# Gathering each expert's tokens with the residual's columns as the stationary operand, in a two-block fp32 network

## What is computed

```python
cap = EC_CAPACITY_FACTOR * n // N_EXPERTS            # 2 * 256 / 16 = 32 tokens for each expert
logits = h @ w_router + b_router
aff = softmax(logits)
gate, idx = top_k(swapaxes(aff, 1, 2), cap)
xs = h[idx]                                          # gather: 16 x 32 rows of 1024
a = einsum('becd,edf->becf', xs, w_gate)             # w_gate, w_up: 1024 x 2048 for each expert
u = einsum('becd,edf->becf', xs, w_up)
y = einsum('becf,efd->becd', silu(a) * u, w_down) * gate
out = zeros.at[idx].add(y)                           # scatter back to the 256 tokens
```

## Time and profile before

| | us |
|---|---|
| median of 3 runs (1554.5 to 1554.9) | 1554.64 |
| the profiled execution, in all | 1554.04 |
| its span from first to last instruction | 1552.2 |
| TensorE busy in the span | 1198.4 (77%) |
| TensorE's weight loads | 696.7 (45%) |
| VectorE | 614.4 (40%) |
| ScalarE | 425.8 (27%) |
| read from memory | 548.36 MB, 354 GB/s over the span |

### The profile page before, as it was taken

The page is one execution under the profiler, slowest core; times in us unless marked ns, Lnnn a source line. Parts: engine busy times, 40 slices in busy tenths (PEclk is TensorE's granted clock), DMA queues, the critical chain, the costliest instruction groups (busy, mean ns, idle before and its releaser), DMA issues.

```text
span 1552.2 us, 18204 instructions
## 1 busy us (share of the span) xinstructions
PE 1198.4 (77%) x7368; PEld 696.7 (45%) x7368; DVE 614.4 (40%) x1041; ACT 425.8 (27%) x644; POOL 36.9 (2%) x62
## 2 busy tenths in 40 slices
PE   7999999999999999976666665665655665665665
PEld 5888977887887899721111111111111111111112
DVE  3786789889777876511011011011011011110111
ACT  3665357786554674300000000000000000000001
POOL 0000000010001000000000000000000000000000
PEclk9999999999999999988777787787878877777788
DMA  9876877687756666999999999999999999999996
GB/s 362 284 263 216 308 245 246 231 307 235 273 183 209 215 220 245 390 432 430 430 432 430 430 431 432 430 432 432 432 429 431 432 430 431 431 430 430 432 432 276
DMA packets 78323, 550.62 MB, mean 355 GB/s; under 512 B 5032, under 2 KB 5320, under 8 KB 61856
## 3 DMA queue, kind: packets, MB, share of 16 engines
q1 hardware_dynamic: 75168, 541.08, 86.2%
q0 software_dynamic: 2784, 8.08, 1.7%
q10 hardware_dynamic: 288, 0.30, 0.1%
HBM read 548.36 MB, written 1.61 MB: 354 GB/s over the span
## 4 chain that ended last, share of the span: by engine, by line
PE 43%; DMA 36%; DVE 12%; ACT 4%; issue 3%; SPq 0%; DVEq 0%; ACTq 0%; POOL 0%
PE ps L610 41%; DMA b<-in_w_down 34%; DVE b L1535 6%; ACT b L1171 3%; PE ps L614 3%; DVE b L1552 2%; DVE b L2265 1%; ACT b L1173 1%; DVE b L2206 1%; DMA b<-in_w_in 1%; DMA b<-in_w_ada 1%; DVE b L2212 1%; DVE b L1545 0%; ACT L1171 0%; DVE b L1566 0%
## 5 line engine op out<-in xcount | busy, mean ns | idle before, releaser
L610 PE MATMUL ps<-b,b 128*32 128x512 f32 (+7 forms) x6922 | 1130.3, 541 | 300.0 <-DMA b<-in_w_up 117.3
L610 PEld LDWEIGHTS ps<-b,b 128*32 128x32 f32 (+2 forms) x6922 | 640.9, 159 | 750.5 <-issue 456.5
L1171 ACT ACTIVATE b<-ps 128x512 f32<-128x512 f32 (+3 forms) x165 | 92.2, 559 | 868.7 <-PE ps L610 560.7
L1535 DVE TENSOR_TENSOR b<-b,b 128x1024 fp32r<-128x1024 f32 (+5 forms) x254 | 277.1, 1091 | 98.1 <-ACT b L1171 78.9
L1171 ACT ACTIVATE b<-b 128x1024 fp32r<-128x1024 f32 (+6 forms) x219 | 219.1, 1001 | 213.9 <-PE ps L610 161.2
L2255 DVE TENSOR_TENSOR b<-b,ps 128x512 f32<-128x512 f32 x16 | 11.0, 687 | 395.6 <-issue 382.3
L2265 DVE TENSOR_TENSOR b<-b,ps 128x1024 f32<-128x1024 f32 x28 | 34.2, 1222 | 304.3 <-PE ps L610 304.3
L614 PE MATMUL ps<-b,b 128*128 128x128 f32 (+1 forms) x360 | 69.7, 322 | 38.4 <-DVE b L1566 23.5
L614 PEld LDWEIGHTS ps<-b,b 128*128 128x128 f32 (+1 forms) x360 | 45.8, 168 | 88.9 <-DVE b L1566 36.4
L1552 DVE SCALAR_TENSOR_TENSOR b<-b,b,b 128x512 f32<-128x512 f32 (+3 forms) x50 | 63.2, 1263 | 4.3 <-ACT b L1171 0.5
L1535 DVE TENSOR_TENSOR b<-ps,b 128x512 f32<-128x512 f32 (+8 forms) x69 | 37.6, 545 | 26.5 <-PE ps L610 14.9
(11 more groups left out here) (59 smaller groups left out, 201.0 us busy)
## 6 DMA issues: line engine op xcount, KB each, us to landing
b<-in_w_up SPq DMA_DIRECT2D x30, 4096.0 KB, 43.2
b<-in_w_gate SPq DMA_DIRECT2D x29, 4096.0 KB, 43.0
b<-in_w_down SPq DMA_DIRECT2D x29, 4096.0 KB, 38.5
b<-in_w_in SPq DMA_DIRECT2D x73, 1024.0 KB, 5.6
b<-in_w_ada SPq DMA_DIRECT2D x28, 1024.0 KB, 5.5
b<-in_w_gate SPq DMA_DIRECT2D x6, 2048.0 KB, 9.0
b<-in_w_down SPq DMA_DIRECT2D x5, 2048.0 KB, 13.0
b<-in_w_ada SPq DMA_DIRECT2D x16, 512.0 KB, 11.4
```

The source lines that it names most:

```text
L610: return e.matmul(o, lhsT, rhs, start=start, stop=stop, skip_group_check=True)
L1171: e.activation(o, i, f, bias=bias, scale=scale).then_inc(mark[0], 1)
L1535: e.tensor_tensor(o, a, b, op).then_inc(mark[0], 1)
```

## The change

The gather changes its operands. Stationary is now the residual: for each token half t, half b and quarter j, 128 of its columns with a step of four values. Moving is the half of ONE with its 32 slots. The result has the 1024 columns on the partitions and the slots beside each other, which is what the flips of XS made. Eight matmuls become sixteen; ScalarE's copy to XS and the two flips of XS are gone, with the semaphores p_gath and a_xs; the flips of Z follow the gather; VectorE's wait before the next row comparison is for p_xt.

```diff
-                    for j in range(4):
-                        ins = mm(ps[32 * j:32 * j + 32, 0, 0:T].rearrange("p (q l) -> p q l", l=2), ONE[:, t, :],
-                                 XC[:, t, j // 2, j % 2], t == 0, t == NT - 1)
-                ins.then_inc(S("p_gath"), 1)
+                    for b in range(2):
+                        for j in range(4):
+                            o = ps[:, 0, T + b * P + j * CAP:T + b * P + (j + 1) * CAP]
+                            ins = mm(o, XC[:, t, j // 2, j % 2, :, b], ONE[:, t, :], (t, b, j) == (0, 0, 0), t == NT - 1)
+                ins.then_inc(S("p_xt"), 1)
                 e.wait_ge(S("v_sel2"), x + 1)
                 for t in range(NT):
                     ins = flip(ps[:, 1, t * P:(t + 1) * P], Z[:, t, :])
                 ins.then_inc(S("p_zt"), 1)
-                e.wait_ge(S("a_xs"), x + 1)
-                for b in range(2):
-                    ins = flip(ps[:, 0, T + b * P:T + (b + 1) * P], XS[:, b::2])
-                ins.then_inc(S("p_xt"), 1)
...
             for x in range(NE):
-                e.wait_ge(S("p_gath"), x + 1)
-                copy(XS, ps[:, 0, 0:T], to=S("a_xs"))
...
                 if x:
-                    e.wait_ge(S("p_gath"), x)
+                    e.wait_ge(S("p_xt"), x)
```

More of the change, by code:

```diff
@@ L427, in build @@
         HD, HTT, YS = at(98, W), at(100, 4, P), at(102, W)
-        AFFR, Z, XS, XT, GT = at(106, NT, P), at(107, NT, P), at(108, T), at(109, 2, P), at(110, T)
+        AFFR, Z, XT, GT = at(106, NT, P), at(107, NT, P), at(109, 2, P), at(110, T)
         junk = [at(106 + i, T) for i in range(4)]
```

## The result

| | before | after |
|---|---|---|
| median, 5 runs each | 1554.9 us | 1561.76 us |
| lowest to highest | 1554.5 to 1557.61 us | 1561.03 to 1563.59 us |
| ratio, 95% interval | | 1.0042 (1.0031 to 1.0052) |
| profiled execution: span | 1552.2 us | 1561.2 us |

The change makes the kernel slower by 0.42%, some 6.5 us (4.8 to 8.1 us by the interval). Forecast were +2 us, and 1555.2 to 1559.4 us as the range: the sign was right, the size was not, and the time lies outside the range.

A forecast was written before the change was run, and what follows sets the result against it. The prediction took the DMA to bound the expert loop, movable only at expert 0's empty queue. Adding 1.99 us to the 1552.2 us span gave 1554.2 us, with time around it 1556.6 us; range 1555.2 to 1559.4 us.

The forecast's parts named there:

- Where the change acts: At expert 0, where the DMA queue is empty: any delay of p_use 1 is added to the end.
- Removed work, 2.16 us: Expert 0, from first gather matmul to VectorE's mix: old gather, copy and flips of XS, 2.16 us in all.
- what hides what: Expert 0: flips of Z run beside VectorE's 0.58 us; its changed wait is long passed; ScalarE's lost copy counts zero.
- the lower end: Expert 0's gather with every load at the router's 0.111 us: 3.77 us, +1.6 us.
- The price of a stepped load: Expert 0's new gather: 0.12 us for each further record, taken from flips of HD; 4.15 us to the mix.
- The sum: Whole kernel: +1.99 us at expert 0, zero from later experts; span 1554.2 us, time 1556.6 us.
- Rival (b): Expert 0's gather: stepped loads dearer than flips show, 0.169 us each, +3.4 us, 1558.0 us; chance 0.08.
- The upper end of the sum: Expert 0's gather with every load paced as the first two stepped flips, 0.22 us: 7.15 us, +5.0 us.
- Rival (a): Expert 0: clock falls under 1.00 before p_use 1, chunk 0 at half speed; +3.7 to +4.9 us in all; chance 0.2.
- Later experts: Experts 1 to 15: gathers up to 5.1 us longer each, hidden by queued pairs and waits for in_w_up; zero at the end.
- the bound of 8.3 us: Experts 1 to 15, new gather at clock 0.50: at most twice its full-clock price, 2 x 4.15 = 8.3 us.
- The waits for in_w_up: TensorE in later experts: these waits shrink by 3 to 5 us each without a change of DMA rate.

The follow-up runs named there:

- e1: New gather in expert 0 alone, old gather, copy and flips kept in experts 1 to 15; 1563.35 us, ratio 1.0044 against the kernel before.
- e2: Old gather in expert 0, new gather in experts 1 to 15; 1554.61 us, ratio 0.9996 against the kernel before.
- e4: Kernel before plus unread extra matmuls ahead of the gathers of experts 2 to 14, testing steps, flips and operand widths; 1554.83 us, one run.
- e7: Kernel before plus unread extra matmuls in later experts, testing other steps, flips and 256 moving columns; 1554.83 us, one run.
- e6: Kernel before plus 24 identity matmuls directly behind expert 0's old gather; 1561.06 us against 1556.07 us, ratio 1.0036.
- e3: Changed kernel with 128 neighbouring residual columns as weights instead of every fourth, results wrong; ratio 1.0014, +2.2 us against the kernel before.
- e5: Changed kernel, but expert 0's gather streams 128 identity columns instead of 32 of ONE, results wrong; ratio 1.0029, +4.5 us against the kernel before.

## Why the prediction was right or wrong

- **Where the change acts: right.** It was read from the chain, the queue and the fading DMA that only p_use 1 of expert 0 counts. e1 and e2 show it by themselves, the table's last column shows it to 0.5 us (0.8 us with e4 and e7), and e6 shows the factor of one.
- **Removed work, 2.16 us, and what hides what: right.** Nothing appeared behind the flips of Z, VectorE's wait or the removed copy; e3's +1.60 us is the lower end, which contained all these terms.
- **The price of a stepped load: wrong, and the main cause.** The sum took 0.12 us for a record, from the flips of HD, "since it is the same size of load with the same step". It measured 0.233 us. The failing step is that a flip stood as witness for a matmul: e4 has both with the same data, size and step, 0.121 us against 0.233 us. The term from the gather's start to the mix was 4.15 us and measured 7.66 us, 3.5 of the 5.1 us by which the sum of +2.0 us fell short of the +7.1 us in the profile. The other 1.6 us are the clock, which the sum left out.
- **Rival (b) was this mechanism with too small a price and too small a chance** (+3.4 us, 0.08): it added the extra length of one load to the router's pace. The upper end of the sum, 0.22 us for each record, came from the first two flips with a step and was put aside because of the third and fourth; it is close to the measured 0.233 us, but that counts as luck: nothing here shows that the two have one cause, and twelve flips of step 4 in e4 settle at 0.121 us as well. The rule in the Trainium skill, Advanced Engine Details and Errata, SBUF Cachelines, two hits for each 16-byte line, spoke against the change and was right for matmuls: 0.118 us at two values for a line, 0.173 us at a step of three, 0.233 us at one value for a line. For flips the runs contradict it (0.121 us at a step of four, 0.111 us at eight). In this case the penalty is a factor of two at the full clock.
- **Rival (a), the clock: it happened**, at +1.6 us, which was its lower price (+1.7 us), and it was given a chance of 0.2. The 1.2 us for a slowed end of the gather did not come, since stepped loads don't follow the clock. But it did not come alone. It was enlarged by what (b) did: a gather of 7.6 us leaves the array thinly used for twice the time that was weighed, and e3, with a gather of 3.7 us and the same short streams, kept the clock. The two rivals were treated as alternatives and priced apart, though the longer gather gave the clock more time to fall. Even at the prediction's own prices the two together, 3.4 + 1.7 = +5.1 us, end at 1559.7 us, past the range; as measured they are +7.1 us.
- **Later experts: right in effect, with sizes off.** Each gather took 7.65 us there, from 1.93 us, so the bound of 8.3 us held. It held by luck: it is twice a price that was itself too low by 3.5 us, and the stepped loads, which don't follow the clock, take the same 7.65 us at 0.50 as at 1.00. The waits for in_w_up shrank as said: one piece of 3.35 us at expert 2 (of the kernel after below) where the earlier trace rows has 4.34 and 3.51 us.

```profile
801.08 7.65 PE L610 MATMUL ps<-b,b 128*128 128x32 f32 x32 [2.05 <-DVE b L2218]
...
825.95 6.58 PE L610 MATMUL ps<-b,b 128*32 128x512 f32 x32 [3.35 <-DMA b<-in_w_up]
...
1513.02 15.34 PE L610 MATMUL ps<-b,b 128*32 128x512 f32 x102 [0.23 <-DVE b L2241]
1530.07 3.64 PE L610 MATMUL ps<-b,b 128*32 128x512 f32 x32 [1.71 <-DMA b<-in_w_up]
```

At expert 15, where the earlier trace rows had 2.72 and 4.17 us of waiting for in_w_up, the first of them is gone and 1.71 us of the second is left: the tail was covered, and narrowly, as the prediction said.

## What to carry to other kernels

In a stage bound by transfers, look for the moment at which the queue is empty: there every microsecond of compute is paid one to one, and elsewhere none is as long as queued transfers cover it, so the same instruction cost all in one place and nothing that could be resolved in fifteen others. Before making a stepped view the stationary or the moving operand of an fp32 matmul, count the values that lie in 16 bytes; with one of them the operand took twice its time at the full clock, and a transposition of the same view is no witness for it. When one rival would make another likelier, price them together.

## What the runs showed of the hardware that was not expected

- An fp32 matmul's weights with a step of 16 bytes load at 1.8 ns for a column (0.233 us for 128) at either clock, against 0.111 us contiguous at a clock of 1.00 and 0.213 us at 0.50; steps of 20 and 32 bytes took 0.220 and 0.238 us. The moving operand pays the same at 1.00, 0.451 us for 256 columns against 0.216 us.
- Flips of the same views do not pay: 0.109 to 0.121 us at steps of 1 to 8 values.
- With a stepped load, 128 moving columns cost no more than 32 (0.233 us both), and with the wider stream the granted clock stayed at 1.00 in the one trace of it (e5), where it fell to 0.50 in both traces with 32 columns (after, e1).
- The time ahead of the experts varies by 2.8 us between profiled executions of the same instructions (651.06 to 653.85 us), more than most of the differences studied here. Counted from the gather's start, the time to the first load repeats to 0.01 us in the four kernels with the same work there (4.81, 4.81, 4.81 and 4.82 us in before, e2, e4 and e7), and the rest to the end to 0.8 us.
